# Two decoder layers on one core: the split input of a first projection, its folded scales and the order of its products

## The reference

```python
for l in range(2):
    sh1, sc1, g1, sh2, sc2, g2 = split(silu(c) @ w_ada[l] + b_ada[l], 6)
    u = x * (1 + sc1) + sh1
    mix = token_mixer(u, ...)      # projections of u, two attentions, gates, branch and output projection
    x = layer_norm(ALPHA * x + (1 + g1) * mix, ln1_g[l], ln1_b[l])
    u = x * (1 + sc2) + sh2
    x = layer_norm(ALPHA * x + (1 + g2) * ((silu(u @ Wa) * (u @ Wb)) @ w_ffn_out[l]), ln2_g[l], ln2_b[l])
```

## Time and profile before

| | |
|---|---|
| median of 3 runs | 1712.31 us (1712.21 to 1713.32) |
| the profiled execution | 1710.0 us |
| its span | 1708.2 us |
| PE busy | 1645.1 us, 96% of the span |
| DVE busy | 1018.2 us, 60% |
| ACT busy | 633.0 us, 37% |
| mean granted TensorE clock | 0.986 |

### The profile page before, as it was taken

The page is one execution under the profiler, slowest core; times in us unless marked ns, Lnnn a source line. Parts: engine busy times, 40 slices in busy tenths (PEclk is TensorE's granted clock), DMA queues, the critical chain, the costliest instruction groups (busy, mean ns, idle before and its releaser), DMA issues.

```text
span 1708.2 us, 21648 instructions
## 1 busy us (share of the span) xinstructions
PE 1645.1 (96%) x8463; PEld 1292.0 (76%) x8463; DVE 1018.2 (60%) x1635; ACT 633.0 (37%) x1151; POOL 50.6 (3%) x100
## 2 busy tenths in 40 slices
PE   6899999999999999999989999999999999999997
PEld 3778666677778888888878776666778788888886
DVE  3677677868676555546567656777567533333344
ACT  3332444545253322222244324455533533222222
POOL 1000000000001000000000000000000000000000
PEclk8999999999999999999989999999999999999997
DMA  9664222134326666665426231110223233333331
GB/s 307 184 179 136 62 66 59 50 89 134 111 62 209 195 188 186 188 183 152 129 66 194 76 87 38 38 38 26 75 86 99 75 98 99 94 94 101 91 102 50
DMA packets 278597, 192.05 MB, mean 112 GB/s; under 512 B 8360, under 2 KB 264928, under 8 KB 278496
## 3 DMA queue, kind: packets, MB, share of 16 engines
q1 hardware_dynamic: 264544, 147.95, 30.0%
q0 software_dynamic: 12032, 42.07, 8.3%
q10 hardware_dynamic: 1920, 0.66, 0.2%
HBM read 188.55 MB, written 2.10 MB: 112 GB/s over the span
## 4 chain that ended last, share of the span: by engine, by line
PE 88%; DVE 6%; DMA 2%; ACT 2%; issue 2%; SPq 0%; ACTq 0%; DVEq 0%
PE banks L1492 24%; PE banks L1494 23%; PE banks L1493 23%; PE banks L1606 4%; PE banks L1634 3%; PE banks L1660 2%; DMA ada_first<-in_w_ada_dram 2%; PE banks L1539 1%; PE banks L1540 1%; PE banks L1541 1%; PE banks L1608 1%; PE banks L1554 1%; PE banks L1694 1%; DVE w_lo L917 1%; PE banks L1666 1%
## 5 line engine op out<-in xcount | busy, mean ns | idle before, releaser
L1492 PE MATMUL banks<-u_hi,w_hi 128*128 128x512 f32 x1216 | 500.6, 412 | 14.9 <-DVE w_lo L917 9.0
L1494 PE MATMUL banks<-u_hi,w_lo 128*128 128x512 f32 x1216 | 476.0, 391 | 0.0
L1493 PE MATMUL banks<-u_lo,w_hi 128*128 128x512 f32 x1216 | 475.9, 391 | 0.0
L917 DVE TENSOR_TENSOR w_lo<-ring,w_hi 128x1024 fp32r<-128x1024 f32 (+2 forms) x246 | 294.4, 1199 | 303.8 <-ACT w_hi L653 302.8
L653 ACT ACTIVATE w_hi<-ring 128x1024 fp32r<-128x1024 f32 (+2 forms) x246 | 253.7, 1032 | 207.0 <-PE banks L1494 103.9
L1492 PEld LDWEIGHTS banks<-u_hi,w_hi 128*128 128x128 f32 x1216 | 229.3, 189 | 69.1 <-issue 14.6
L1494 PEld LDWEIGHTS banks<-u_hi,w_lo 128*128 128x128 f32 x1216 | 229.0, 188 | 49.2
L1493 PEld LDWEIGHTS banks<-u_lo,w_hi 128*128 128x128 f32 x1216 | 230.2, 189 | 36.6
L805 ACT ACTIVATE probs<-banks,neg_max 128x128 f32<-128x128 f32 (+3 forms) x192 | 99.6, 524 | 168.1 <-DVE neg_max L1272 168.1
L1492 PE MATMUL banks<-h_hi,w_hi 128*128 128x512 f32 x352 | 138.5, 394 | 0.0
L1494 PE MATMUL banks<-h_hi,w_lo 128*128 128x512 f32 x352 | 137.0, 389 | 0.0
(11 more groups left out here) (225 smaller groups left out, 2049.6 us busy)
## 6 DMA issues: line engine op xcount, KB each, us to landing
ring<-in_w_ffn_in_dram SPq DMA_DIRECT2D x88, 512.0 KB, 3.9
ada_ring<-in_w_ada_dram POOLq DMA_DIRECT2D x80, 512.0 KB, 4.3
ring<-in_w_in_dram SPq DMA_DIRECT2D x72, 512.0 KB, 3.8
ring<-in_w_ffn_out_dram SPq DMA_DIRECT2D x32, 448.0 KB, 3.6
ada_first<-in_w_ada_dram SPq DMA_DIRECT2D x16, 512.0 KB, 8.3
ring<-in_w_out_dram SPq DMA_DIRECT2D x16, 512.0 KB, 3.8
ring<-in_w_ffn_out_dram SPq DMA_DIRECT2D x16, 512.0 KB, 4.5
w<-in_cmp_w_k_dram SPq DMA_DIRECT2D x8, 512.0 KB, 5.0
```

Source lines behind the costliest of these rows:

```text
L917: V.tensor_tensor(lo, src, hi.bitcast(fp32), ALU.subtract).then_inc(split_lo, 1)
L1492: M(bank, wh[:, block], sh[:, k, :], start=start, stop=False)
L1493: M(bank, wh[:, block], sl[:, k, :], start=False, stop=False)
L1494: return M(bank, wl[:, block], sh[:, k, :], start=False, stop=stop)
```

## The change

Four edits, all around the input of a sub-layer:

1. ACT writes `u_hi` straight from the normed value, with the scale and offset, and after it `raw`, from the same source with the same scale and offset. Before, `raw` came first and `u_hi` was copied from it. A new semaphore `u_raw` tells DVE that `raw` is there.
2. The wait for the `u_lo` of two blocks before now stands between the two ACT instructions.
3. The folded scales are computed by DVE in the layer norm's loop over columns, behind the L1027 of column 5, and no longer between the reciprocal and the first subtraction.
4. `project_first` waits for the high half of a block, issues the two products with it for every name, then waits for the low half and issues the one product with it for every name. This holds for the merged mixer output (`wo0`, `wo1`) as well.

```diff
             def sub_layer_input(n, m, src, scale, bias):
 
+                nc.scalar.activation(u_hi[:, m, :], src, ACT.Identity, bias=bias, scale=scale).then_inc(u_high, 1)
                 if n * KD + m >= 2:
 
                     act.wait_ge(u_ready, n * KD + m - 1)
-                link(nc.scalar.activation(raw[:, m % 2, :], src, ACT.Identity, bias=bias, scale=scale))
-                nc.scalar.activation(u_hi[:, m, :], raw[:, m % 2, :], ACT.Copy).then_inc(u_high, 1)
+                nc.scalar.activation(raw[:, m % 2, :], src, ACT.Identity, bias=bias, scale=scale)\
+                    .then_inc(u_raw, 1)
...
+                    if m == 5 and which == 0:
+                        ada_part2(l)
+                    elif m == 5 and not last_norm:
+                        ada_part1(l + 1)
                     if m == 1:
...
                 V.reciprocal(rstd_s, var_s).then_inc(rstd_saved, 1)
-                if which == 0:
-                    ada_part2(l)
-                elif l + 1 < DEPTH:
-                    ada_part1(l + 1)
                 for m in range(KD + 1):
...
                 dve.wait_ge(u_high, n * KD + m + 1)
+                dve.wait_ge(u_raw, n * KD + m + 1)
                 V.tensor_tensor(u_lo[:, m, :], raw[:, m % 2, :], u_hi[:, m, :].bitcast(fp32), ALU.subtract)\
...
-            def project_first(l, names, src, ready, count):
+            def project_first(l, names, src, high, ready, count):
 
                 w = [take_split(l, name) for name in names]
                 out = [take_bank(l, name) for name in names]
+                sh, sl = src
                 for k in range(KD):
+                    block = slice(k * P, (k + 1) * P)
+                    pe.wait_ge(high, count + k + 1)
+                    for bank, (wh, wl) in zip(out, w):
+                        M(bank, wh[:, block], sh[:, k, :], start=k == 0, stop=False)
+                        M(bank, wl[:, block], sh[:, k, :], start=False, stop=False)
                     pe.wait_ge(ready, count + k + 1)
-                    for i, name in enumerate(names):
-                        last = product(out[i], w[i], src, k, k, k == 0, k == KD - 1)
+                    for name, bank, (wh, wl) in zip(names, out, w):
+                        last = M(bank, wh[:, block], sl[:, k, :], start=False, stop=k == KD - 1)
                         if k == KD - 1:
                             done(l, name, last)
```

More of the change, by code:

```diff
@@ L379, in build @@
         u_high = sem("u_high")
+        u_raw = sem("u_raw")
         mix_high = sem("mix_high")
@@ L1749, in _ @@
                 if l:
-                    project_first(l, FIRST, (u_hi, u_lo), u_ready, 2 * l * KD)
+                    project_first(l, FIRST, (u_hi, u_lo), u_high, u_ready, 2 * l * KD)
                 project(l, "kwn")
@@ L1811, in _ @@
                         done(l, f"y{a}{m}", last)
-                project_first(l, ("wo0", "wo1"), (merged_hi, merged_lo), merged, l * KD)
+                project_first(l, ("wo0", "wo1"), (merged_hi, merged_lo), merged_high, merged, l * KD)
                 for m in range(2, KD):
@@ L1817, in _ @@
                     if f == 0:
-                        project_first(l, ("fa0", "fb0", "fa1"), (u_hi, u_lo), u_ready, (2 * l + 1) * KD)
+                        project_first(l, ("fa0", "fb0", "fa1"), (u_hi, u_lo), u_high, u_ready, (2 * l + 1) * KD)
                     else:
```

## The result

The changed kernel takes 1718.85 us (median of 8 runs, 1716.4 to 1719.24) against 1712.51 us for the kernel before (8 runs beside it, 1711.05 to 1714.05). The ratio is 1.0032, with a 95% interval of 1.0023 to 1.0041: slower by 5.5 us (3.9 to 7.0). The forecast was 1712.8 us, with 1715.8 us as the upper end of the range, so the result lies outside it. The profiled execution took 1716.4 us with a span of 1714.6, 6.4 us more than that of before. It is the shortest of the eight, so the trace shows a mild case of the loss.

The account below looks back on a forecast made before the run. PE, busy 1645.1 of 1708.2 us, was taken to set the end nearly everywhere. The terms, -1.86 - 1.36 + 2.73 + 0.91 + 0.07 = +0.5 us, on a median of 1712.31 gave 1712.8 us, range 1709.8 to 1715.8.

Parts of the forecast that it names:

- Term 3: Ends of the groups of three: the first name ends 0.91 us later, adding idle before fb1 twice and kwn: +2.73 us.
- the third rival: Longer idle before fb1 lowers the clock: slower, two falls giving 1716.2 to 1717.8 us; chance 0.13.
- Term 1: Start behind the first norm, clock full: PE starts at 493.18 and not 495.04, a gain of 1.86 us.
- terms 1 and 2: Earlier PE starts behind the norms: 1.86 us in the first, 1.36 us in the second and third at half clock.
- all three at half (0.6 to 0.8 each) makes it +1.7: Unknown size: with all three inner norms at half clock, each gains 0.6 to 0.8 us and the sum becomes +1.7.
- Term 4: Merged input: wo0's last product comes 0.45 us later, adding idle before wo2 in both layers: +0.91 us.
- Term 5: Folding at column 5: some 0.5 us of DVE, hidden in its 1.05 us of idle before the next column's update.
- Term 6: Layer 0's first projections: the low half of block 7 comes about 0.07 us later and PE waits: +0.07 us.
- The whole gain arrives: Rival: terms 3 and 4 vanish; 1709.2 us with the clock as profiled, 1706.8 with it full in all norms; chance 0.10.
- All norms at the full clock: Rival: all three inner norms run at full clock, the sum is -1.9 and the time 1710.4 us; chance 0.15.

Follow-up runs that it names:

- experiment 4: Kernel before, with the last block in the new order only for fa0, fb0 and fa1, in both layers: 1716.9 us, ratio 1.0027.
- experiment 1: Changed kernel with the last block of each first projection in the old order, name by name: 1712.03 us, ratio 0.9993.
- experiment 3: Kernel before, with the last block in the new order only for the pair wo0 and wo1: 1713.45 us, ratio 1.0001.
- experiment 8: Changed kernel with the old product order in every block; direct `u_hi` and moved folding stay: 1713.68 us, ratio 1.0001.
- experiment 2: Kernel before, with only the last block of each first projection in the new order: 1718.28 us, ratio 1.0030.
- experiments 6 and 7: Unread products added in PE's waits before fb1 and kwn: on the changed kernel 1716.9 us; on the kernel before with all last blocks in new order 1716.2 us.
- experiment 11: Kernel before, with only the third name's last three blocks (of the pair: wo1's last two) issued last: 1708.38 us, ratio 0.9973.

## Why the prediction was wrong

**Term 3 failed: it priced the longer wait before fb1 as idle time alone.** The idle is as forecast, 1.66 to 2.57 twice and 4.32 to 5.22, and so is its cause. But the wait of 2.57 us also brings the clock down. That was the third rival, with a chance of 0.13, and for the two falls it gave 1716.2 to 1717.8; the measured 1718.85 lies beyond even that. The fourteen profiled executions (the two kernels' and the twelve above) show how PE's idle before fb1 or kwn and the clock behind it go together:

| idle | low stretch behind it |
|---|---|
| none to 1.83 us | 0 of 26 |
| 2.57 us | 4 of 6 |
| 2.93 and 2.96 us | 2 of 2 |
| 4.3 to 5.2 us | 8 of 8 |

Each fall behind fb1 is 3.4 us at half the clock, 1.7 us lost by the count of the clock. With 4 of 6 that makes 2 x 0.67 x 1.7 = 2.3 us for the two places, where term 3 had 0. With the idle of 1.8 it makes 4.1, and experiment 4 measured 4.6 by the ratio and 4.0 between the medians. The earlier trace rows gave a full clock behind 1.66 and a low one behind 4.32, and 2.57 lies between. Nothing in the profile made the full clock the likelier there, and for an unknown size between two rows of opposite outcome 0.13 was too low.

**Term 1 failed in its condition: the clock at full in the first norm.** The profiled execution of before had it, but it is the exception. The duration of the eight fillers tells the clock in a norm: 2.10 us there, and 2.8 to 3.8 us in the other 41 of the 42 norms in the fourteen executions. So the fillers hold PE until after `u_hi` is there, and terms 1 and 2 together are worth what experiment 1 shows, 1.2 us (2.6 gained to 0.3 lost), and not 3.2. The text named this size ("all three at half (0.6 to 0.8 each) makes it +1.7") and left it out of the forecast. In the changed kernel's own profiled execution 0.36, 0.40 and nothing were gained where 1.86, 0.59 and 0.77 were expected.

With both mended the sum is 0.5 + 2.0 + 2.3 = 4.8 us, against 5.5 (3.9 to 7.0) measured. Both corrections are sized from the experiments, so this agreement is a check of the account and no forecast. The range stopped at one fall on top of the sum with all norms at half, 1715.8, although the rival beyond it had been worked out.

**What held.** Term 4: idle before wo2 of 0.71 and 0.78 us as forecast; experiment 3 finds +0.2 us, with -1.4 to +1.5 around it, so the trace shows the 0.9 and the clock of the device can't. Term 5: the folding is hidden; DVE's idle before column 6's update is 0.54 us in place of 1.05, and experiment 8 finds no loss. Term 6: PE's two waits for `u_lo` in the last blocks of layer 0's first projections are 0.86 and 0.38 us against 0.80 and 0.37, 0.07 more, as forecast; the kernel was 0.1 us late already ahead of them. Kept as well: the input stays ahead of PE inside the groups, and PE keeps its program order: fa0's low product starts at 511.01, behind all six high ones. By the rule of the Trainium skill ("TensorE: Matmul & The Clock Gate", "Part 2: What happens when you issue a matmul"), that matmuls stay in program order, this was to be expected. The trace agrees, with that row and with 11.6 us of waiting for `w_lo` against 9.0.

The direct `u_hi` takes 0.82 us, the copy took 0.63, so the 0.81 that the sum went by was right. The prediction read the skill's page as making the two equal, and that reading was wrong. The Trainium skill ("ScalarE: Activation LUTs", "What ACT_TABLE_LOAD costs") states 186 ns and 0.833 ns per element with immediate scale and bias, and about 93 ns more for each of the two that comes from a column; an estimate from these figures for 512 elements is 0.61 us for the copy and 0.80 for the direct `u_hi`. The trace agrees with both. The equal throughput of all functions, which the prediction cites, is per element and leaves this fixed part out.

**The other rivals.** "The whole gain arrives" is refuted by experiment 2: the wait behind the group moves with the first name's end. "All norms at the full clock" did not occur in any of the fourteen executions.

**What stays open.** Why 2.57 us brings the clock down in some cases and not in others; the changed kernel has both in one execution (0.50 us products behind the wait at both, a low stretch behind the first only). The traces hold a hint. In the four cases with a fall the norm ahead of the group had been at the low clock for 3.4 us (in the changed kernel 0.66 over 5 us, which is 2 x 0.34 x 5), in the two without a fall for 6.8 us (0.57 over 8). So what the clock did in the norm seems to bear on the fall behind the group; six cases do not show it, and with waits of 1.66 us neither kind of norm was followed by a fall. How often the first norm of the kernel before has the full clock was seen in one profile only, so what terms 1 and 2 would be worth in a typical execution rests on experiment 1. And the fillers of experiments 6 and 7 gave back less than the clock that they kept; the waits for later splits explain some 1.8 us of it in the trace, but this was not isolated, and where the clock of their slower executions was lost is not known. Not tried was the changed kernel with fewer fillers in the norms, although in its trace they are what keeps PE from `u_hi`.

## What to carry to other kernels

When products of several results are reordered, ask first who waits for the first result and how late it becomes; hiding an input's latency at the head of a group is worth nothing if the same reorder delays the release at its tail. The last result is the one to put off: its products cover the wait (experiment 11). Price an idle stretch of PE that grows beyond the longest one with a full clock behind it as idle plus a fall of the clock, and take the clock seen in one profiled execution as one sample, reading a fixed group of products as the gauge.

## What the hardware showed

- The fall of the clock can come late: in the changed kernel the wait ended at 514.42, and only the products from 515.7 on were slow; in experiment 4 the first product behind the same wait already took 0.79. A full-speed first product behind a wait does not show that the wait was harmless, and the prediction read it so for 1.66 us (rightly there, 0 falls in 10 places).
- At the end of a norm the clock was down in 41 of 42 cases. In the changed kernel's first norm PE had 4.9 us of transposes and products of one column there (486.95 to 491.87) with one named wait, of 0.38 us, and then the eight fillers.
- Faster products moved waits from one split to the next (0.75 and 1.0 us behind kwn in experiments 6 and 7, in place of 0.2 in experiment 2): behind kwn the weight splits on ACT and DVE have little room left once PE keeps its clock.
